# Split products in the latent attention, and the weight sums' copies issued beside the mixer's output

## The reference

```python
cq  = rms_norm(z[..., :256], q_norm)
ckv = rms_norm(z[..., 256:384], kv_norm)
k_pe = apply_rope(z[..., 384:], cos, sin)                       # 64 wide, one for all heads
q  = (cq @ w_qb).reshape(B, L, 8, 128 + 64)                     # q_nope, q_pe (rotated)
kv = (ckv @ w_kvb).reshape(B, L, 8, 128 + 128)                  # k_nope, v
s  = (q_nope @ k_nope^T + q_pe @ k_pe^T) * scale                # causal, then softmax
o  = softmax(s) @ v
```

## Time and profile before

| | us |
|---|---|
| median of 3 runs | 2647.94 |
| profiled execution | 2652.91 |
| its span | 2651.1 |
| latent attention, PE's first product to DVE's last hand-over | 1470.28 to 1593.61 |
| one head in its steady part | 14.55 |
| PE busy over the span | 2476.3 (93%) |
| DVE busy | 1789.7 (68%) |
| ACT busy | 1184.2 (45%) |

### The profile page before, as it was taken

The page is one execution under the profiler, slowest core; times in us unless marked ns, Lnnn a source line. Parts: engine busy times, 40 slices in busy tenths (PEclk is TensorE's granted clock), DMA queues, the critical chain, the costliest instruction groups (busy, mean ns, idle before and its releaser), DMA issues. The chain is left out here.

```text
span 2651.1 us, 33685 instructions
## 1 busy us (share of the span) xinstructions
PE 2476.3 (93%) x13175; PEld 1970.2 (74%) x13175; DVE 1789.7 (68%) x2553; ACT 1184.2 (45%) x1668; POOL 87.7 (3%) x184
## 2 busy tenths in 40 slices
PE   7999899999999999899988899998999989999996
PEld 5666678777777878788875457887888977788885
DVE  4899545587775666899965565675766574665557
ACT  5444422255564225588853343621324244365443
POOL 0000000000000000100001000000000000000001
PEclk9999999999999988999999999999999899999998
DMA  7887727333235744999962213598861414243446
GB/s 264 263 286 268 249 83 282 85 104 95 80 104 178 259 73 159 346 419 420 417 267 92 67 37 104 144 241 239 241 175 48 154 28 143 64 159 121 134 157 168
DMA packets 312398, 478.29 MB, mean 180 GB/s; under 512 B 29195, under 2 KB 198654, under 8 KB 302385
## 3 DMA queue, kind: packets, MB, share of 16 engines
q1 hardware_dynamic: 285392, 409.29, 45.4%
q0 software_dynamic: 22320, 57.67, 8.3%
q10 hardware_dynamic: 4528, 9.18, 0.9%
HBM read 431.82 MB, written 74.69 MB: 191 GB/s over the span
## 5 line engine op out<-in xcount | busy, mean ns | idle before, releaser
L2380 DVE TENSOR_TENSOR expert_parts<-w,expert_parts 128x2048 fp32r<-128x2048 f32 x102 | 232.6, 2288 | 21.2 <-ACT expert_parts L2376 20.8
L1345 PE MATMUL banks<-h_parts,ssm_parts 128*128 128x512 f32 x960 | 230.2, 397 | 0.8 <-DVE ssm_parts L1612 0.4
L3761 PE MATMUL banks<-big,late_parts 128*128 128x512 f32 x960 | 222.6, 394 | 5.7 <-DVE late_parts L3914 5.7
L2376 ACT ACTIVATE expert_parts<-w 128x2048 fp32r<-128x2048 f32 x102 | 194.7, 1916 | 60.2 <-PE banks L2387 51.8
L3761 PEld LDWEIGHTS banks<-big,late_parts 128*128 128x128 f32 x960 | 182.2, 190 | 45.2 <-issue 4.9
L1345 PEld LDWEIGHTS banks<-h_parts,ssm_parts 128*128 128x128 f32 x960 | 179.5, 189 | 43.7 <-issue 6.7
L2387 PE MATMUL banks<-expert_parts,expert_xt 128*128 128x512 f32 x816 | 192.1, 395 | 4.0 <-DVE expert_xt L2368 4.0
L2387 PEld LDWEIGHTS banks<-expert_parts,expert_xt 128*128 128x128 f32 x816 | 153.5, 190 | 36.4 <-DVE expert_xt L2368 4.7
L3761 PE MATMUL banks<-h_parts_second,late_parts 128*128 128x512 f32 x720 | 167.5, 393 | 7.5 <-DVE late_parts L3914 5.1
L3761 PEld LDWEIGHTS banks<-h_parts_second,late_parts 128*128 128x128 f32 x720 | 136.7, 190 | 36.6 <-issue 8.0
L4176 PE MATMUL banks<-h_parts_second,late_parts 128*128 128x512 f32 x512 | 159.4, 393 | 2.4 <-DVE h_parts_second L4406 2.4
(11 more groups left out here) (791 smaller groups left out, 4729.6 us busy)
## 6 DMA issues: line engine op xcount, KB each, us to landing
w_second<-in_mlp_w_dram SPq DMA_DIRECT2D x60, 1024.0 KB, 5.4
w<-in_w_exp_gate_dram SPq DMA_DIRECT2D x34, 1024.0 KB, 9.3
w<-in_w_exp_up_dram SPq DMA_DIRECT2D x34, 1024.0 KB, 9.0
w<-in_w_exp_down_dram SPq DMA_DIRECT2D x34, 1024.0 KB, 9.0
w<-in_w_in_dram SPq DMA_DIRECT2D x64, 512.0 KB, 4.6
w<-in_mod_mix_w_dram SPq DMA_DIRECT2D x24, 1024.0 KB, 5.1
down_sums<-in_mlp_w_dram POOLq DMA_DIRECT2D x6, 4096.0 KB, 31.3
w<-in_mod_ffn_w_dram SPq DMA_DIRECT2D x23, 1024.0 KB, 6.1
```

What stands on the lines that cost most here:

```text
L1345: mm = pe.matmul(ps[:, t % 2, :], parts[:, t % SPLITS, w, kk, :], k.hp[:, x, kk, :], start=(kk == 0 and j == 0), stop=(kk == KD - 1 and j ...
L2376: act.activation(self.high_part(h), self.raw(h), ACT.Copy).then_inc(self.high_done, 1)
L2380: dve.tensor_tensor(self.low_part(h), self.raw(h), self.high_part(h).bitcast(F32), ALU.subtract).then_inc(self.low_done, 1)
L3761: mm = pe.matmul(ps[:, bank(n, f), :], w_part(n, w)[:, kk, f * P:(f + 1) * P], x[:, v, kk, :], start=(first_chunk(n) and kk == 0 and j == ...
```

## The change

In the latent attention queries, keys and scores become split products; values, transposes and the products with the values stay. The raw rotated query's high and low part are stacked on 128 partitions against a doubled copy of the high part of `k_pe`, so two of the three rotated terms are one product. The new tiles lie in the unused half of a large buffer (`room`). The core of the diff (definitions, renamed semaphores and the passing of arguments left out):

```diff
 # PE
+            def projection(out, w, x):
+                for c in range(u.nq):
+                    for j, (a, v) in enumerate(split):
+                        mm = pe.matmul(out, w(a, c), x(v)[:, c, :], start=(c == 0 and j == 0), stop=(c == u.nq - 1 and j == 2))
             def rope_query(i):
-                pe.wait_ge(s[f"w_loaded{i % 2}"], 32 * (i // 2 + 1))
+                pe.wait_ge(s["w_low"], i + 1)
...
             def key(i):
                 pe.wait_ge(s["rotated"], i + 1)
-                pe.matmul(ps[:, 7, :], u.wkv[:, i % 2, 0:NOPE], ckv[:], start=True, stop=True).then_inc(s["kn_done"], 1)
+                for j, (a, v) in enumerate(split):
+                    mm = pe.matmul(ps[:, 7, :], u.wk_parts[:, i % 2, a, :], u.ckv(v), start=(j == 0), stop=(j == 2))
...
-                pe.matmul(ps[:, g % 3, 0:n], u.qn[:, i % 2, n - P:n], u.kn[:, i % 2, 0:n], start=True, stop=False)
-                pe.matmul(ps[:, g % 3, 0:n], u.qp[:, i % 2, n - P:n], k_pe[:, 0:n], start=False, stop=True).then_inc(s["scores_done"], 1)
+                for j, (a, v) in enumerate(split):
+                    pe.matmul(ps[:, g % 3, 0:n], u.qn(i, a)[:, n - P:n], u.kn(i, v)[:, 0:n], start=(j == 0), stop=False)
...
+                pe.matmul(ps[:, g % 3, 0:n], u.qp_both[:, i % 2, n - P:n], u.k_pe(0)[:, 0:n], start=False, stop=False)
+                pe.matmul(ps[:, g % 3, 0:n], u.qp_both[0:ROPE, i % 2, n - P:n], u.k_pe(1)[:, 0:n], start=False, stop=True).then_inc(s["scores_done"], 1)
 # ACT, loop over g
                 copy_turned(g)
                 if n == 0 and i + 1 < H:
-                    copy_key(i + 1)
+                    key_high(i + 1)
                 if n == 1 and i + 1 < H:
                     copy_value(i + 1)
                 if g + 2 < last:
                     exponent(g + 2)
+                if n == 1 and i + 2 < H:
+                    weights_high(i + 2)
                 if n == 3 and i + 2 < H:
-                    copy_query(i + 2)
+                    rope_high(i + 2)
+                    query_high(i + 2)
 # DVE, loop over g
+                if n == 0 and i + 1 < H:
+                    key_low(i + 1)
                 if g + 1 < last:
                     normalise(g + 1)
                 if g + 2 < last:
                     row_max(g + 2)
                 if n == 0 and i:
                     hand_over(i - 1)
+                if n == 1 and i + 2 < H:
+                    weights_low(i + 2)
                 if n == 2 and i + 2 < H:
-                    rotated(i + 2)
+                    rope(i + 2)
+                if n == 3 and i + 2 < H:
+                    rope_low(i + 2)
+                    query_low(i + 2)
```

The weight sums:

```diff
 # residual_stage, POOL, behind router.widen
+            k.sums.copy(pool)
 # WeightSums
-    def form(self, pool, products, every):
+    def copy(self, pool):
+        for n, (odd, half) in enumerate(((0, 0), (0, 0), (0, 1), (1, 0))):
+            pool.dma_start(self.total(n), self.block(odd, half)).then_inc(self.copied, 16)
+
+    def form(self, pool, products):
         two, three, right, four = (self.total(n) for n in range(4))
-        n = 0
-        for dst, first, then in ((two, self.block(0, 0), self.block(0, 1)), (three, two, self.block(1, 1)),
-                                 (right, self.block(0, 1), self.block(1, 1)), (four, three, self.block(1, 0))):
-            for src, op in ((first, ALU.bypass), (then, ALU.add)):
-                pool.wait_ge(products, every * (n + 2))
-                pool.dma_start(dst, src, accum_op=op).then_inc(self.formed, 16)
-                n += 1
-                pool.wait_ge(self.formed, 16 * n)
+        pool.wait_ge(self.copied, 64)
+        for n, (dst, src, behind) in enumerate(((two, self.block(0, 1), 12), (right, self.block(1, 1), 20), (three, right, 28), (four, three, 54))):
+            pool.wait_ge(products, behind)
+            pool.dma_start(dst, src, accum_op=ALU.add).then_inc(self.formed, 16)
+            pool.wait_ge(self.formed, 16 * (n + 1))
```

More of the change, by code:

```diff
@@ L3374, in copy_query, with rope_high, key_high @@
                     act.wait_ge(s["scores_done"], TB * (i - 1))
-                act.activation(u.qn[:, i % 2, :], ps[:, 6, :], ACT.Copy, scale=scale).then_inc(s["qn_copied"], 1)
-            def copy_key(i):
+                act.activation(u.qn(i, 0), ps[:, 6, :], ACT.Copy, scale=scale).then_inc(s["qn_high"], 1)
+            def rope_high(i):
+                act.wait_ge(s["qp_ready"], i + 1)
+                if i >= 2:
+                    act.wait_ge(s["scores_done"], TB * (i - 1))
+                act.activation(u.qp_both[0:ROPE, i % 2], u.qp[:], ACT.Copy).then_inc(s["qp_high"], 1)
+            def key_high(i):
                 act.wait_ge(s["kn_done"], i + 1)
@@ L3401, in copy_turned @@
                 act.activation(u.pt[:, g % 2, 0:n], ps[:, 3 + g % 2, 0:n], ACT.Copy).then_inc(s["turned_copied"], 1)
-            copy_query(0)
-            copy_key(0)
+            act.activation(u.cq(0), cq[:], ACT.Copy).then_inc(s["in_high"], 1)
+            weights_high(0)
+            act.activation(u.ckv(0), ckv[:], ACT.Copy).then_inc(s["in_high"], 1)
+            act.activation(u.k_pe(0)[0:ROPE], k_pe[:], ACT.Copy).then_inc(s["in_high"], 1)
+            query_high(0)
+            rope_high(0)
+            key_high(0)
+            weights_high(1)
             copy_value(0)
@@ L3407, in _ @@
             exponent(1)
-            copy_query(1)
+            query_high(1)
+            rope_high(1)
             for g in range(last):
@@ L3423, in _, with weights_low, rope, rope_low @@
             step = Steps(dve, s["rope_step"])
-            def rotated(i):
-                dve.wait_ge(s["qp_done"], i + 1)
[L3427 to L3430, removed]
+            def weights_low(i):
+                dve.wait_ge(s["w_high"], 2 * i + 2)
+                dve.tensor_tensor(u.wk_parts[:, i % 2, 1], u.wkv[:, i % 2, 0:NOPE], u.wk_parts[:, i % 2, 0].bitcast(F32), ALU.subtract)
+                dve.tensor_tensor(u.wq_parts[:, i % 2, 1], u.wq[:, i % 2], u.wq_parts[:, i % 2, 0].bitcast(F32), ALU.subtract).then_inc(s["w_low"], 1)
+            def rope(i):
+                dve.wait_ge(s["qp_done"], i + 1)
+                rotate(step, dve, u.qp, ps[0:ROPE, 7, :], u.raw, u.swapped, cos, sin, scale, s["qp_ready"])
+            def rope_low(i):
+                dve.wait_ge(s["qp_high"], i + 1)
+                dve.tensor_tensor(u.qp_both[ROPE:2 * ROPE, i % 2], u.qp[:], u.qp_both[0:ROPE, i % 2].bitcast(F32), ALU.subtract).then_inc(s["rotated"], 1)
+            def query_low(i):
+                dve.wait_ge(s["qn_high"], i + 1)
+                dve.scalar_tensor_tensor(out=u.qn(i, 1), in0=ps[:, 6, :], scalar=scale, in1=u.qn(i, 0).bitcast(F32), op0=ALU.mult,
+                                         op1=ALU.subtract).then_inc(s["qn_low"], 1)
+            def key_low(i):
+                dve.wait_ge(s["kn_high"], i + 1)
+                dve.tensor_tensor(u.kn(i, 1), ps[:, 7, :], u.kn(i, 0).bitcast(F32), ALU.subtract).then_inc(s["kn_low"], 1)
             def row_max(g):
@@ L3452, in hand_over @@
                 dve.tensor_tensor(o_parts[:, 1, i, :], ps[:, 5, :], high.bitcast(F32), ALU.subtract).then_inc(s["o_low"], 1)
-            rotated(0)
+            dve.wait_ge(s["in_high"], 1)
+            dve.tensor_tensor(u.cq(1), cq[:], u.cq(0).bitcast(F32), ALU.subtract).then_inc(s["in_low"], 1)
+            weights_low(0)
+            dve.wait_ge(s["in_high"], 2)
+            dve.tensor_tensor(u.ckv(1), ckv[:], u.ckv(0).bitcast(F32), ALU.subtract).then_inc(s["in_low"], 1)
+            dve.wait_ge(s["in_high"], 3)
+            dve.tensor_copy(u.k_pe(0)[ROPE:2 * ROPE], u.k_pe(0)[0:ROPE].bitcast(F32)).then_inc(s["pe_twice"], 1)
+            dve.tensor_tensor(u.k_pe(1), k_pe[:], u.k_pe(0)[0:ROPE].bitcast(F32), ALU.subtract).then_inc(s["in_low"], 1)
+            rope(0)
+            query_low(0)
+            rope_low(0)
+            key_low(0)
+            weights_low(1)
             row_max(0)
@@ L3457, in _ @@
             normalise(0)
-            rotated(1)
+            rope(1)
+            query_low(1)
+            rope_low(1)
             for g in range(last):
                 i, n = g // TB, g % TB
+                if n == 0 and i + 1 < H:
+                    key_low(i + 1)
                 if g + 1 < last:
@@ L3754, in _ @@
             pool.wait_ge(s["x_low"], KD)
-            later.form(pool, s["tile_done"], 3 * HT)
+            later.form(pool, s["tile_done"])
         @block.tensor
@@ L5405, in second_block @@
     glu_stage(k, g, high_half, low_half, k.ins["ssm_w_out_2"][0], parts)
-    closing_stage(k, 1, k.ins["ssm_w_out_2"][0], low_half, big, parts, sums, out)
+    closing_stage(k, 1, k.ins["ssm_w_out_2"][0], low_half, big, parts, k.sums, out)
 def build(nc, ins, out):
@@ L5425, in build @@
             router = Router(k)
+            k.sums = WeightSums(k, "down_sums", k.ins["mlp_w2_2"][1])
```

70 lines of the change are left out of this document (48 added, 22 removed).

## The result

The kernel after takes 2694.62 us, the median of 4 runs (2690.13 to 2702.88), against 2649.02 for the kernel before in the same runs: ratio 1.0172, 95% interval 1.0141 to 1.0203. The forecast was 2669.7, or +21.8; measured is +45.6. The sign was right, the slowdown is more than twice the one forecast, and 2694.6 lies just inside the stated range of 2652 to 2695, at its very end.

A forecast was written before the change was run, and what follows sets the result against it. PE, busy 93% of the span, was taken as the bound. Attention +26.6, copies +4 and tail -8.8 gave +21.8 on 2647.9: 2669.7 us, likeliest case 2660 to 2683, range with rivals 2652 to 2695.

The forecast's parts named there:

- The copies' cover: Four 4 MB copies beside the mixer's output end near 1037 and delay the routing's both_b: +4 us, range 0 to +10.
- The chain of the latent attention: Latent attention: waits from queue to queue make a head 17.9 us against 14.55, +24.1 us with start and end.
- the 1.1 us for steps: Latent attention: about 31 steps of 35 ns between neighbouring instructions add 1.1 us to a head's sum of 16.8.
- rival B: Latent attention: the clock falls in both gaps of each head, 13 us in place of 2.5, total 2680; chance 0.17.
- The tail: Tail: only one adding transfer meets the stores, loss 4.8 in place of 13.6 us: -8.8, range -4 to -13.6.
- Rival D: Tail: stores still meet transfers that wait for one another, stalls stay at 8.6 us; +8.8, total 2678.5; chance 0.07.
- Rival A (the other side): Latent attention: slack hides the pairs, DVE's own work bounds the head at 13.6 us; -10.9, total 2637; chance 0.09.
- Rival C: Routing: the copies starve its loads, both_b 10 us late, +8.9 in place of +4, total about 2675; chance 0.10.

The follow-up runs named there:

- experiments 2 and 3: Kernel before with the new sums, copies reissued: sums_sp from SP's queue, 2661.75 us; sums_split over two stages, 2646.49; sums_one_last with the second copy late, 2662.76.
- attn_order: attn_only with its operations reordered, such as weights_high one step earlier on ACT, against the kernel before: 2648.93 us, ratio 0.9986.
- sums_split: Kernel before plus the new sums, two copies issued by POOL in the mixer's output and two in the latent stage: 2646.49 us, ratio 0.9984.
- sums_late: Kernel before plus the new sums, all four copies in the latent attention behind its second head's weights: 2655.81 us, ratio 1.0015.
- all_marks: attn_order with the copies of sums_split and adding marks moved to 12, 18, 54, 60, against the kernel before: 2635.10 us, ratio 0.9929.
- attn_only: Kernel after with the weight sums formed as before and no copies, against the kernel before: 2669.81 us, ratio 1.0069.
- sums_only: Kernel before plus the new weight sums, four copies issued by POOL in the mixer's output: 2678.36 us, ratio 1.0109.
- sums_sp: As sums_only, but SP's queue issues the four copies at the end of the mixer's output: 2661.75 us, ratio 1.0046 against the kernel before.
- sums_one_last: As sums_split, but the second copy in the mixer's output is held until about 1013: 2662.76 us, ratio 1.0043 against the kernel before.

## Why the prediction was wrong

- **The copies' cover (the step that failed).** I worked out that 6 MB would still be moving when the routing starts, took it for a slower `both_b` and wrote +4, range 0 to +10. Measured for that stretch: +26.7 at the stage's end and +3.0 behind it; the `both_b` of the forecast landed in 5.1 us. That the copies end near 1037 was in my text, and the routing starts near 1016 in the trace of before, but I did not ask whether an engine may leave a stage with transfers under way. POOL may not (experiments 2 and 3). The answer could be read in the trace of before, in the stage in which POOL gathers the experts' rows:

```profile
1403.12 1.51 POOL L3029 DMA_INDIRECT expert_parts_plain<-expert_rows,slots  x1 [0.30 <-issue]
```

```profile
L151 POOLq DRAIN  x1: 12463/12463/12463, 1397.5 to 1397.5; - x1
```

  POOL's last gather is issued by 1404.6 and lands at 1409.56; its `DRAIN` lasts to 1409.92. It cost nothing there, as the other engines work until 1426, so no row of idle time points at it. As a bound, 1037 less 1016 is 21 us. With that and the 3 us behind it in place of the +4, the same sum gives 2690. How `both_b` shares the DMA with such copies, which the +4 was about, stays untested: in no run does it run beside POOL's.
- **The chain of the latent attention.** Forecast 17.9 a head and +24.1, and +2.5 for the clock; measured 17.07 to 18.28 a head and +22.8 in the trace, clock included. The terms without the 1.1 us for steps sum to 16.8. Taking out what the low clock cost (next point) leaves 16.8 in each steady head, so the terms were right in sum and the steps were not: neighbouring records on DVE overlap. Two more errors nearly cancel in the sum: the copy of the second head's key is 6.1 us late in place of 3.5 (the clock was low for 17 of the 26 us ahead of it), and the stage's end costs 3 us less than forecast. As a median the attention part costs 19.3.
- **The clock (rival B)** came true in part. I had weighed whether it falls in both gaps of each head (13 us) or mostly not (2.5). It fell once or twice in every head. From the first of `rope_query`'s products to the rotation it is 2.31, 2.65 and 2.86 us in three heads and 1.63 in the next three; from `key`'s first product to its copy it is 1.30 us in four and 1.00 where the clock is full, as in `attn_order`. Up to the last key's copy that adds up to 4.1 us.
- **The tail.** Forecast -8.8, within -4 to -13.6; measured -4.9 in the trace after. Over the tables themselves (1765 to 1860) it is -6.5, as in `sums_split`; 1.6 go ahead of them, where the clock fell once more at 1714. `sums_late` has -5.2. The one stall that I had placed at the store of 1779 came, 4.5 us in place of 3.1. Rival D is out; `all_marks` shows the whole of what there was to gain, 12.9 us between the two ends of the tail (13.6 in the text).
- **Rival A (the other side)** was near in its numbers and wrong in its condition: it had 13.6 us a head as what DVE's own work allows, and `attn_order` reaches 13.46. The change as written is not in that state, as `weights_low` and `rope_low` wait for ACT 1.5 and 1.1 us a head.

That 2694.6 lies inside the range is luck. Rival C, at the same place, has `both_b` land late, and it landed on time; no rival held what happened.

Open: the 3.1 us between `y_scaled(0)` and the latent stage. They are not the copies': `attn_only`, which has none, shows 2.8 there, and `sums_only`, `sums_sp` and `sums_one_last` 2.7, 2.4 and 1.4, while `all_marks` shows none. No run tells what they are.

## What to carry to other kernels

Before a transfer is put beside a stage, compare the time at which it lands with the time at which the stage ends; if POOL issued it, the difference is idle time of every engine. No busy row names it; the sequencer's rows at the line that closes the stage do. In a trace of before, look there for a long `DRAIN`, even one that costs nothing yet. Where an operation is split into a high and a low part on two engines, draw the chain from queue to queue and take each wait out by moving the high part ahead of the long wait on its queue: DVE busy for 71% and ACT for 40% of a head say nothing of this. And a transfer in a quiet stretch still delays small loads that run beside it.

## What was not expected of the hardware

- POOL's `DRAIN` at a stage's end lasts until its own transfers have landed (to 1041.14 for a landing at 1040.92, to 1030.38 for one at 1030.25), and all engines wait for it; SP's lasts 0.37 us with two copies under way that land 12.4 and 25.7 us later.
- SP's queue took long to issue large copies from DRAM to DRAM: the four 34.73 us, and the two loads of 512 KB behind them 10.43 (0.81 in the kernel after). POOL issued its four in 4.20 us.
- A load of 192 KB beside POOL's copies landed in 10.2 us in place of 2.5.
